# The cosines and sines of the scan are formed in the last eight down-projected chunks of the first feed-forward

## The reference

```python
h2 = rms_norm(x, g_ffn)
x = x + (jax.nn.silu(h2 @ w_gate) * (h2 @ w_up)) @ w_down      # end of the first layer
...
h = _rms(x, norm1_w[l]) * (1 + sc1) + sh1                      # second layer
proj = h @ w_in[l]
...
dt = jnp.exp(log_dt.astype(f32))[:, None]                      # inside _s5
mag = jnp.exp(dt * lr)
a_re = mag * jnp.cos(dt * li)
a_im = mag * jnp.sin(dt * li)
...
_, _, s_re, s_im = lax.associative_scan(combine, (a_re_t, a_im_t, bu_re, bu_im), axis=1)
```

## Time and profile before

| | us |
|---|---|
| median of 3 runs | 1281.24 |
| lowest and highest | 1281.05, 1283.07 |
| profiled execution, first to last instruction | 1279.9 |
| last eight down-projected chunks, each | 7.48 |
| seam, from the end of chunk 7 to the first multiplication of the mixer | 14 |

### The profile page before, as it was taken

How to read it: one execution, slowest core, us unless ns; L and a number is a source line. 1 busy time by engine, 2 the same in 40 slices (tenths; PEclk the granted TensorE clock), 3 DMA queues, 4 the chain that set the end, 5 groups by cost and what they waited for, 6 DMA issues and landing times. The chain is left out here.

```text
span 1279.9 us, 15375 instructions
## 1 busy us (share of the span) xinstructions
PE 1226.4 (96%) x6230; PEld 964.2 (75%) x6230; DVE 762.1 (60%) x1224; ACT 485.6 (38%) x738; POOL 125.2 (10%) x124
## 2 busy tenths in 40 slices
PE   7999998999999999999997998789899999999998
PEld 5786675577888888888885885467688878888877
DVE  5536675755666855656645976946756652455542
ACT  5244545734323212222224714564433331333320
POOL 0000000023000900000011920014200000000000
PEclk9999999999999999999998998999999999999999
DMA  9311011223543365444442331102122223322222
GB/s 348 131 56 66 34 66 54 79 99 99 173 168 124 115 210 186 162 170 152 126 173 94 67 84 34 67 1 99 66 99 99 78 73 124 104 99 99 68 91 89
DMA packets 25829, 138.40 MB, mean 108 GB/s; under 512 B 2879, under 2 KB 5152, under 8 KB 16544
## 3 DMA queue, kind: packets, MB, share of 16 engines
q1 hardware_dynamic: 25760, 137.43, 31.9%
HBM read 133.75 MB, written 3.67 MB: 107 GB/s over the span
## 5 line engine op out<-in xcount | busy, mean ns | idle before, releaser
L133 PE MATMUL bank<-xhi_ffn,w_hi_part 128*128 128x512 f32 x704 | 277.8, 395 | 4.4 <-DVE xlo_ffn L233 4.4
L134 PE MATMUL bank<-xlo_ffn,w_hi_part 128*128 128x512 f32 x704 | 276.9, 393 | 0.0
L121 ACT ACTIVATE w_hi_part<-w_raw 128x2048 fp32r<-128x2048 f32 (+1 forms) x96 | 165.9, 1728 | 289.8 <-PE bank L135 288.1
L135 PE MATMUL bank<-xhi_ffn,w_lo_part 128*128 128x512 f32 x704 | 275.0, 391 | 0.0
L127 DVE TENSOR_TENSOR w_lo_part<-w_raw,w_hi_part 128x2048 fp32r<-128x2048 f32 (+1 forms) x96 | 198.4, 2067 | 111.1 <-ACT w_hi_part L121 106.9
L133 PEld LDWEIGHTS bank<-xhi_ffn,w_hi_part 128*128 128x128 f32 x704 | 132.7, 189 | 34.7 <-issue 5.4
L135 PEld LDWEIGHTS bank<-xhi_ffn,w_lo_part 128*128 128x128 f32 x704 | 132.7, 188 | 29.5
L134 PEld LDWEIGHTS bank<-xlo_ffn,w_hi_part 128*128 128x128 f32 x704 | 132.5, 188 | 27.8 <-issue 0.2
L360 DVE SCALAR_TENSOR_TENSOR squares<-bank,param,squares 128x511 f32<-128x511 f32 x88 | 63.9, 747 | 84.0 <-ACT squares L343 82.4
L133 PE MATMUL bank<-hhi,w_hi_part 128*128 128x512 f32 x240 | 94.5, 394 | 1.7 <-DVE hlo L368 1.7
L133 PE MATMUL bank<-hhi_half,w_hi_part 128*128 128x512 f32 x240 | 94.1, 392 | 0.7 <-DVE hlo_half L332 0.7
(11 more groups left out here) (363 smaller groups left out, 1926.4 us busy)
## 6 DMA issues: line engine op xcount, KB each, us to landing
mod_w<-in_w_mod SPq DMA_DIRECT2D x32, 768.0 KB, 4.4
w_raw<-in_w_gu SPq DMA_DIRECT2D x22, 1024.0 KB, 4.8
w_raw<-in_w_down SPq DMA_DIRECT2D x32, 704.0 KB, 4.0
w_raw<-in_w_up SPq DMA_DIRECT2D x22, 1024.0 KB, 4.9
w_raw<-in_w_in_f SPq DMA_DIRECT2D x8, 1024.0 KB, 5.3
w_raw<-in_w_out SPq DMA_DIRECT2D x8, 1024.0 KB, 4.8
w_raw<-in_w_in SPq DMA_DIRECT2D x5, 1024.0 KB, 5.0
x<-in_x SPq DMA_DIRECT2D x8, 256.0 KB, 6.7
```

Source lines behind the costliest of these rows:

```text
L121: act.activation(k.whi[:, slot, 0:width], k.raw[:, slot, 0:width], ACT.Copy).then_inc(k.w_hi, 1)
L133: pe.matmul(out, whi, xhi, start=first, stop=False)
L134: pe.matmul(out, whi, xlo, start=False, stop=False)
L135: return pe.matmul(out, wlo, xhi, start=False, stop=last)
```

## The change

The four batches move from the mixer into chunks 0 to 6 of the last eight. The order on ACT is now: chunk 0, `turns(0)` and `turns(1)`; chunk 1, `turns(2)` and `turns(3)`; chunks 2 to 5, `sines(0)` to `sines(3)`, each behind the weights that are rounded in that chunk. On DVE: in chunk 1 a copy of the step numbers to a bank, and in chunks 1 to 4 `angle(0)` to `angle(3)`, in chunks 3 to 6 `cosine(0)` to `cosine(3)`, each behind the modulation's multiplications. The results and the angles lie over tiles of the up-projections' input, which is dead by then. The load of `time` moves to the start of the feed-forward. The table load for logarithm and exponential moves from chunk 0 to behind `sines(3)` in chunk 5, the one ahead of the mixer's second weight chunk goes, and so does the one in the mixer. The sines in the feed-forward are taken from the table set that is loaded for its up-projections.

```diff
@@ block.sync, feed-forward
+                sp.dma_start(time[:, :], io["time"]).then_inc(time_in, 16)
                 for n in range(GU, IN2 + 4):
@@ block.scalar, feed-forward (turns and sines as in the mixer before, on other tiles)
                     for j in range(KT):
                         if half == 1:
-                            if j == 0:
-                                act.preload_act_table_set("natural_log_exp_and_others")
                             act.wait_ge(ffn.added, KT + j + 1)
                             r3.act_square(act, k, x[:, j, :], j)
                         if half == 0 or j < KT - 1:
                             ffn.act_weights(act, ffn.down_chunk(half, j) + 2)
+                        if half == 1:
+                            if j == 0:
+                                act.wait_ge(time_in, 16)
+                                act.wait_ge(col_den, 2)
+                                turns(0)
+                                turns(1)
+                            if j == 1:
+                                turns(2)
+                                turns(3)
+                            if 2 <= j < 6:
+                                sines(j - 2)
+                            if j == 5:
+                                act.preload_act_table_set("natural_log_exp_and_others")
                 r3.act_root(act, KT, eps_col[:, 0:1])
-                act.preload_act_table_set("trig_and_small")
+                own.act = chain.n
                 ffn.act_weights(act, ffn.down_chunk(1, KT - 1) + 2)
@@ block.vector, feed-forward (angle and cosine as in the mixer before, on other tiles)
                         modulation.multiply(dve, modulation.DOWN)
+                        if half == 1:
+                            if j == 1:
+                                dve.wait_ge(time_in, 16)
+                                dve.wait_ge(a_moved, 2)
+                                dve.tensor_copy(clock, chunk_time).then_inc(time_set, 1)
+                                dve.wait_ge(time_set, 1)
+                            if 1 <= j < 5:
+                                angle(j - 1)
+                            if 3 <= j < 7:
+                                cosine(j - 3)
@@ block.tensor, feed-forward
+                pe.wait_ge(angled, 4)
                 r3.pe_sum(pe, k, KT - 2, [KT - 1])
@@ block.scalar, mixer
-                act.wait_ge(c_in, 32)
-                act.wait_ge(h3_split, KT)
-                turns(0)
-                turns(1)
                 act.wait_ge(k.w_used, IN2 + 1)
                 first_tile(IN2, 0, k.bank[0])
                 next_weights(IN2 + 2)
...
-                sines(0)
...
-                sines(1)
                 first_tile(IN2 + 1, 2, k.bank[0])
-                turns(2)
-                turns(3)
                 next_weights(IN2 + 3)
-                sines(2)
-                sines(3)
-                act.preload_act_table_set("natural_log_exp_and_others")
@@ block.vector, mixer
-                dve.wait_ge(c_in, 32)
-                dve.tensor_copy(clock, chunk_time).then_inc(time_set, 1)
-                dve.wait_ge(time_set, 1)
-                angle(0)
-                angle(1)
                 second_tile(IN2, 1)
                 next_rest(IN2 + 2)
-                cosine(0)
-                cosine(1)
-                angle(2)
-                angle(3)
                 second_tile(IN2 + 1, 3)
                 next_rest(IN2 + 3)
-                cosine(2)
-                cosine(3)
```

More of the change, by code:

```diff
@@ L1354, in program @@
             k.sem(f"ssm_{w}") for w in ("b_in", "exponents", "sines", "denominator", "inverse", "wide", "turned", "rows"))
+        time_in, time_set, turned, angled, sined, half_sined, circled = (
+            k.sem(f"circle_{w}") for w in ("time_in", "time_set", "turns", "angles", "sines", "half_sines", "cosines"))
+        time = over("time", [P, S], time_at)
+        angles = over("angles", [P, 4, S], o_at)
+        half_sines = over("half_sines", [P, 2, S], o_at + 4 * TILE)
+        circle = over("cos_sin", [P, 16, 2, NCK], circle_at)
+        chunk_time = time[:, :].rearrange("p (c t) -> p c t", t=TS)[:, :, 0]
+        clock = k.bank[6][:, 0:NCK]
         def col(n):
@@ L1647, in _, with angle, cosine @@
                 dve.wait_ge(r2.inverted, 1)
+                def angle(b):
+                    ang = angles[:, b, :]
+                    dve.wait_ge(turned, b + 1)
+                    for part, op in ((TH_HI, ALU.subtract), (TH_LO, ALU.add)):
+                        for q in range(4):
+                            a = ang[:, NCK * q:NCK * q + NCK]
+                            mark = chain.mark(dve.scalar_tensor_tensor(
+                                out=a, in0=clock, scalar=col(part)[:, 4 * b + q:4 * b + q + 1], in1=a,
+                                op0=ALU.mult, op1=op))
+                        chain.need(mark)
+                    dve.tensor_scalar(ang, ang, 0.5, -0.5, ALU.min, ALU.max).then_inc(angled, 1)
+                def cosine(b):
+                    dve.wait_ge(half_sined, b + 1)
+                    half_sine = half_sines[:, b % 2, :].rearrange("p (t c) -> p t c", c=NCK)
+                    dve.tensor_scalar(circle[:, 4 * b:4 * b + 4, 0, :], half_sine, -2.0, 1.0, ALU.mult, ALU.add)\
+                        .then_inc(circled, 1)
                 for half in range(2):
@@ L1662, in _ @@
                                                      op1=ALU.mult)
+                own.dve = chain.n
                 ffn.dve_weights(dve, ffn.down_chunk(1, KT - 1) + 2)
@@ L1834, in program @@
         root_a, root_b = k.root, square_sum
[L1836 to L1837 removed]
+        hot_in, rel_made, rel_sb, rel_out, rel_in, c_taken = (
+            k.sem(w) for w in ("hot_in", "rel_made", "rel_copied", "rel_out", "rel_in", "ssm_c_taken"))
         h3_scaled, h3_rounded, h3_split = k.sem("in2_scaled"), k.sem("in2_rounded"), k.sem("in2_split")
[L1839 to L1841 removed]
+        evac2a, evac2v, half_made, c_in, bt_made, bt_sb, lifted = (
+            k.sem(w) for w in ("in2_stored_a", "in2_stored_v", "in2_half", "ssm_c_in", "b_turned", "b_copied", "c_lifted"))
         h2_sq, h2_sum, h2_root, h2_inv, h2_wide, h2_scaled, h2_done = (
@@ L1852, in program @@
                                           "turned", "moved", "summed", "stored"))
-        chunk_time = time[:, :].rearrange("p (c t) -> p c t", t=TS)[:, :, 0]
-        clock = k.bank[6][:, 0:NCK]
         y_bank = k.bank[6]
```

67 lines of the change are left out of this document (22 added, 45 removed).

## The result

| | before | after |
|---|---|---|
| median of the runs, us | 1281.74 (1280.23 to 1283.07, 18 runs) | 1284.36 (1282.22 to 1286.20, 18 runs) |
| profiled span, us | 1279.9 | 1282.5 |

The ratio is 1.0018, with a 95% interval of 1.0012 to 1.0025: 2.3 us slower (1.5 to 3.2), where +1.4 was forecast. By the measure of the prediction (0.2%, 2.6 us) that is within no change, on the slow side; the interval itself excludes zero.

A forecast was written before the change was run, and what follows sets the result against it. The prediction took the kernel as a chain of PE work, busy 96% of the span. PE's stops of 3.3 us, less 1.4 for the table load and 0.5 for a mixer wait, gave +1.4 us: 1282.6, range 1279.6 to 1286.2.

The forecast's parts named there:

- Additions to `x`: Last eight chunks: DVE's serial chain of 4.20 us, multiplications and moved batches makes additions 2 to 5 late.
- PE's stops: Chunks 6 and 7: PE waits about 1.6 us ahead of each for late weights, 3.3 us in sum.
- Prices of clamp and cosine: DVE in the chunks: clamp 0.43 us and cosine 0.45, the cheap prices, as POOL is mostly idle there.
- the rival with dear prices: Clamps 0.77 us and two cosines 1.35 in the chunks; PE loses 6.8 us, median 1286.1; chance 17 in 100.
- The table load: Seam: removing the load ahead of the last rounding takes 1.4 us off the chain ACT, DVE, barrier.
- PE's end at the seam: Seam: PE ends 3.0 us ahead of DVE, so it does not take over as the barrier's last arrival.
- PE's wait in the mixer: Mixer, at 707.84: PE's 0.53 us wait for ACT's copy of the first bank goes, gain 0.5 us.
- The sum: Whole kernel: 3.3 - 1.4 - 0.5 = +1.4 us, median from 1281.24 to 1282.6.
- The clock as a rival: PE's two stops make the granted clock fall, costing 1.7 to 5 us: 1284.3 to 1287.6; chance 13 in 100.

The follow-up runs named there:

- e3: Changed kernel with DVE's moved work spread over other chunks and all four cosines behind the last addition to `x`: 1280.34 us, 0.9990 of the kernel before.
- e5: Kernel before, with POOL's mixer work held back until the fourth cosine is made: 1285.45 us in one run (kernel before on that chip 1281.77).
- e1: Kernel before, with the sine table load put behind the rounding of the mixer's second weight chunk: 1281.36 us, 0.9993 of the kernel before.
- e4: Changed kernel with both removed table loads put back, ahead of the last rounding and in the mixer: 1284.94 us, 1.0023 of the kernel before.
- before_again: Kernel before, unchanged, run once more for a second profile: 1285.26 us in one run.
- e10: Changed kernel itself, timed again on another occasion: 1286.36 us in 5 runs, 1.0037 of the kernel before.
- e8: Changed kernel plus idle PE products at the seam, one behind each of six reduction groups and nine behind the barrier: 1283.13 us, 1.0009 of the kernel before.

## Why the prediction was right, and where its size was off

- **Additions to `x`.** Forecast for additions 2 to 5, counted from x0 at 626.29 before: 16.8, 25.3, 34.5 and 43.7. Measured from x0: 16.74, 25.11, 34.13, 43.16. The chain of 4.20 us, three multiplications and a batch was right to 0.2 us a chunk, and the differences add up to 0.5.
- **PE's stops.** 1.6 us each forecast, 1.10 and 1.23 measured, with both firsts at 0.50 instead of 0.39 us. Chunk 7's addition moved by 55.31 - 52.37 = 2.94 us against 3.3. The whole of it went in e3, where the same work stands in other places: shown.
- **Prices of clamp and cosine.** The cheap ones were right (0.43 and 0.42), so the rival with dear prices fell. e5 shows the reason: the same operations in the old place cost this as soon as POOL is idle. The rival was also priced too high in its clamps: the prediction took 0.77 for all four, while two of the four in the mixer had been cheap (0.44 and 0.43). And the 3.23 us of POOL that the prediction set beside the cosines lay for the most part beside DVE's rest.
- **The table load.** -1.4 forecast, -1.2 in the changed kernel (-1.4 in its two other profiles), -1.4 in e1, +1.3 when put back in e4: shown. The prediction said that PE's end at the seam does not take over, being 3.0 us ahead. In the first profile it did, by 0.2 us, because the reductions ran in part at the half clock.
- **PE's wait in the mixer.** -0.5 forecast. The wait is gone, and F to I gained 0.03 us. **This is the step that failed.** The wait of 0.53 was in none of the other executions in that size: not in before_again, and 0.24 us at 707.37 in e5, though ACT's order there is that of before. It hung on how fast PE came there, and so on how much of the low clock lay behind F. Where little of it does and the wait is absent, the gain is seen: F to I is 25.66 us in e3, 0.8 less than before. In the first profile of the changed kernel 1.6 us more of the low clock lay behind F, and cost 0.7 us. I had read a wait of one execution as a property of the kernel, and had not asked at which clock the products ahead of it ran.
- **The sum.** 2.94 - 1.21 - 0.03 = +1.70 in place of +1.4. Against the executions of before with x0 to I at 92.91 and 93.46, the three of the changed kernel (94.61, 94.48, 94.89) are 1.0 to 2.0 us longer. That the sum came so near is in part luck: the stops were forecast 0.4 us too long, and the two gains together 0.7 us too large.
- **The clock as a rival.** It did not fall over the two stops (1.00 in the windows from 660 to 674.5), so as I put it the rival fell.
- **The rest of the median.** 2.3 us in the first 18 runs and 4.7 in e10 are more than the schedule's 1.0 to 2.0 above. The rest lies in code that both kernels share and in the clock's stretches there. Identical kernels differ by as much (Z to end 433.85 and 436.29), but not equally often: a mean clock of 0.985 or less in 18 of 24 executions against 17 of 78 says that the changed kernel has the longer stretches more often. The prediction had the clock only as a fall behind the two stops, and had no term for this. Why the change does it stays open; e8, which has the changed schedule and none of these low means, shows that the two stops alone don't bring it.

## What to carry to other kernels

Before work is moved into another stage's idle time, follow the serial chain from one iteration to the next with the work in its exact place: 3.3 us of idle per chunk did not hold 2.65 us of work, since 1.97 of it stood in front of the insertion, and the same work two chunks over, or behind the last addition, was free. Price an operation by a row in which the shared neighbour (here POOL) does what it will do in the new place. Where a stage begins at a low clock, don't count on a sooner start in full: as long as the low stretch does not end sooner, only 0.54 us of each microsecond is kept. And before a microsecond of difference is put down to an edit, compare executions at an equal mean clock, and look at how often each kernel has the lower one.

## What the runs showed of the hardware that was not expected

The clock can fall while PE is busy without a gap, and it does so in some executions only. In e10 (windows, columns as in the earlier trace rows):

```profile
95.00:99.00 4.00, 4.00 (x42) 3.38 (x41) 2.79 (x5) 1.04 (x6) 0.00 (x0) 1.00 0.18 39
99.00:100.00 1.00, 1.00 (x8) 0.45 (x6) 0.43 (x1) 0.00 (x0) 0.00 (x0) 1.00 0.92 377
100.00:103.00 3.00, 3.00 (x9) 2.32 (x10) 2.75 (x10) 0.97 (x3) 0.00 (x0) 0.50 0.41 172
```

PE is busy for all of the time and the granted clock is 0.50 from 100 us on, while the same kernel's first profile has 1.00 there. The wait of 2.11 us behind which the clock stayed at 1.00 in the first profile of before is in before_again too, and there the clock fell:

```profile
218.00:222.00 4.00, 3.62 (x12) 1.42 (x14) 2.17 (x1) 0.33 (x1) 0.00 (x0) 0.57 0.16 29
```

The wait is 2.11 us long there too and ends at 218.38. So that a wait left the clock alone in one execution did not mean that it always does. Each of these two falls is 3.4 us long. At 0.46 us for each microsecond that is an estimated 1.6 us, as much as the change's own effect. The start to x0 of 627.37 and 627.18 us in these two, against 625.2 to 626.3 in the others, fits it.
